# A two-layer hybrid decoder trunk on one core: head output of the MLA pairs in parts, rotary steps in other places, weight splits at another point of ScalarE's order

## The reference

```
h = rmsnorm(x, norm_g[l]) * (1.0 + scale) + shift
(a_q, a_f, a_i, a_g, b_cq, b_ckv, b_kr, b_g,
 c_q, c_k, c_v, c_g, m_a, m_b, m_c) = split_cols(h @ w_in[l])
y_a = hgrn2_mixer(a_q, a_f, a_i, ...) * silu(a_g)
y_b = mla_mixer(b_cq, b_ckv, b_kr, ...) * silu(b_g)
y_c = retention_mixer(c_q, c_k, c_v, ...) * silu(c_g)
merged = sigmoid(m_a) * (y_a @ w_pa[l]) + sigmoid(m_b) * (y_b @ w_pb[l]) + sigmoid(m_c) * (y_c @ w_pc[l])
x = x + gate * (merged @ w_out[l])
```

```
s = (qn @ k_nope^T + qr @ k_rope^T) * scale      # causal, 128 queries at a time
o = softmax(s) @ v
```

## Time and profile before

| | |
|---|---|
| median of 3 runs | 1367.94 us (1367.6 to 1369.93) |
| profiled execution | 1367.47 us |
| its span, first to last instruction | 1365.7 us |
| mean granted clock of TensorE | 0.977 of full speed |
| busy: PE, DVE, ACT, POOL | 94%, 51%, 46%, 53% |
| chain that ended last, by engine | PE 86%, DVE 7%, ACT 3%, issue 2% |

### The profile page before, as it was taken

How to read it: one execution, slowest core, us unless ns; L and a number is a source line. 1 busy time by engine, 2 the same in 40 slices (tenths; PEclk the granted TensorE clock), 3 DMA queues, 4 the chain that set the end, 5 groups by cost and what they waited for, 6 DMA issues and landing times.

```text
span 1365.7 us, 16803 instructions
## 1 busy us (share of the span) xinstructions
PE 1286.3 (94%) x5754; PEld 1013.3 (74%) x5754; DVE 698.4 (51%) x1136; ACT 626.6 (46%) x953; POOL 722.7 (53%) x1471
## 2 busy tenths in 40 slices
PE   5999999899789999999979999989979999999996
PEld 2878887777567777788858888777756687778884
DVE  6767767433655444454364777643354552433333
ACT  4276656434343244454235666544344424435431
POOL 3365555763324654576747654576522364555662
PEclk8999999999999999999989999999999999999998
DMA  9322223342113333233212212233211132232231
GB/s 374 118 84 77 63 67 104 112 146 90 48 62 108 130 102 108 101 124 105 95 55 93 78 62 71 70 99 120 90 47 39 56 130 75 87 99 87 93 93 62
DMA packets 40902, 130.51 MB, mean 96 GB/s; under 512 B 5392, under 2 KB 5520, under 8 KB 39536
## 3 DMA queue, kind: packets, MB, share of 16 engines
q1 hardware_dynamic: 30448, 110.22, 24.6%
q10 hardware_dynamic: 10368, 19.21, 4.4%
HBM read 126.33 MB, written 2.10 MB: 94 GB/s over the span
## 4 chain that ended last, share of the span: by engine, by line
PE 86%; DVE 7%; ACT 3%; issue 2%; POOL 1%; DMA 1%; ACTq 0%; DVEq 0%
PE ps_st L797 21%; PE ps_st L799 20%; PE ps_st L798 20%; PE ps_o L850 6%; PE ps_s L885 2%; PE ps_s L924 2%; PE ps_s L947 1%; PE ps_w L933 1%; POOL w_lo L669 1%; PE ps_misc L845 1%; ACT w_hi L1004 1%; DVE t L1298 1%; DVE neg_max L1709 1%; DVE gate_x L1315 1%; PE ps_w L752 1%
## 5 line engine op out<-in xcount | busy, mean ns | idle before, releaser
L669 POOL TENSOR_TENSOR w_lo<-raw,w_hi 128x128 fp32r<-128x128 f32 x1448 | 710.3, 529 | 602.6 <-ACT w_hi L1004 602.6
L797 PE MATMUL ps_st<-h_hi,w_hi 128*128 128x512 f32 x920 | 372.8, 405 | 2.7 <-POOL w_lo L669 2.2
L799 PE MATMUL ps_st<-h_hi,w_lo 128*128 128x512 f32 x920 | 359.0, 390 | 0.0
L798 PE MATMUL ps_st<-h_lo,w_hi 128*128 128x512 f32 x920 | 358.5, 390 | 0.0
L1004 ACT ACTIVATE w_hi<-raw 128x1024 fp32r<-128x1024 f32 x182 | 190.2, 1046 | 81.4 <-PE ps_st L799 51.9
L797 PEld LDWEIGHTS ps_st<-h_hi,w_hi 128*128 128x128 f32 x920 | 172.9, 188 | 44.8 <-issue 5.8
L798 PEld LDWEIGHTS ps_st<-h_lo,w_hi 128*128 128x128 f32 x920 | 173.0, 188 | 38.5 <-issue 4.8
L799 PEld LDWEIGHTS ps_st<-h_hi,w_lo 128*128 128x128 f32 x920 | 172.6, 188 | 36.9
L1315 DVE TENSOR_SCALAR gate_x<-ps_st 128x512 f32<-128x512 f32 x79 | 54.5, 690 | 219.7 <-PE ps_st L799 219.1
L1026 ACT ACTIVATE gate_t<-gate_x 128x512 f32<-128x512 f32 x80 | 50.5, 631 | 249.5 <-DVE gate_x L1315 249.5
L850 PE MATMUL ps_o<-mla_pt,v_ones 128*128 128x512 f32 (+3 forms) x128 | 46.4, 513 | 18.6 <-issue 10.2
(11 more groups left out here) (309 smaller groups left out, 2022.9 us busy)
## 6 DMA issues: line engine op xcount, KB each, us to landing
raw<-w_stream SPq DMA_DIRECT2D x178, 512.0 KB, 3.5
mod_w<-w_mod ACTq DMA_DIRECT2D x64, 256.0 KB, 2.7
pro_w<-w_mod_first SPq DMA_DIRECT2D x8, 1024.0 KB, 14.3
x<-x_t SPq DMA_DIRECT2D x4, 512.0 KB, 7.4
ret_decay<-decay ACTq DMA_DIRECT2D x2, 1024.0 KB, 5.0
out_t<-o_t SPq DMA_DIRECT2D x8, 256.0 KB, 2.2
raw<-w_stream SPq DMA_DIRECT2D x4, 384.0 KB, 3.2
raw_extra<-w_stream SPq DMA_DIRECT2D x2, 512.0 KB, 20.3
```

What stands on the lines that cost most here:

```text
L669: ins = nc.gpsimd.tensor_tensor(lo[:, r], whole[:, r], hi[:, r].bitcast(F32), ALU.subtract)
L797: nc.tensor.matmul(dst[0:m, :], wh, hi, start=(k == 0), stop=False)
L798: nc.tensor.matmul(dst[0:m, :], wh, lo, start=False, stop=False)
L799: last = nc.tensor.matmul(dst[0:m, :], wl, hi, start=False, stop=(k == nk - 1))
```

## The change

It has these parts.

1. `mixers_first` keeps the split in a list of its own and puts it out when the *next* group is flushed, behind that group's other steps.
2. `mla_pv` is cut for ScalarE and VectorE into `mla_rs` (rstd), `mla_y` (y_t; y_hi on odd heads) and `mla_lo` (y_lo). `mla_rs` of head h-1 stands between the third and fourth exponentials of head h, `mla_lo` behind the maxima of blocks 3 and 2 of a later head.
3. The odd key of a pair is copied in a step `mq_odd` of its own; the even key has a semaphore, `k_even`. PE waits for the even key before an even head's first score and for the odd key before the odd head's.
4. `mr` is read from its bank by a ScalarE copy into sq_sum, and turned by VectorE in a step `mr_rope`, for `mr 1` behind the maxima of head 3. `kr_rope` is done in two halves, one and two merge gates later.

```diff
@@ build_schedule
-    s += [("ckv_norm",), ("kr_rope",)]
-    for it in ma[1:-4]:
+    s.append(("ckv_norm",))
+    for n, it in enumerate(ma[1:-4]):
         item(*it)
+        if n < 2:
+            s.append(("kr_rope", n))
...
         else:
             item("bg", 0)
-        s += [("mla_t", h, 3), ("mla_t", h, 2), ("mla_s", h, 1), ("mla_s", h, 0)]
+        if h % 2 == 1 and h > 1:
+            s.append(("mla_lo", h - 2))
+        if h == 3:
+            s.append(("mr_rope", 1))
+        s += [("mla_t", h, 3), ("mla_t", h, 2)]
+        if h:
+            s += [("mla_rs", h - 1), ("mla_y", h - 1)]
+        s += [("mla_s", h, 1), ("mla_s", h, 0)]
         item(*behind[h])
         s += [("mla_t", h, 1), ("mla_t", h, 0)]
+        if behind[h][0] == "mq":
+            s.append(("mq_odd", behind[h][1]))
@@ mixers_first
-LATER = ("hg_v", "hg_out", "mla_pv", "ret_out")
+LATER = ("hg_v", "hg_out", "mla_y", "ret_out")
...
-            out += [t for t in group if t[0] not in EARLY + LATER + NEXT + ("item",)]
+            out += [t for t in group if t[0] not in EARLY + LATER + NEXT + ("item",)] + split
...
             if i < N_ITEMS and not (layer == 0 and RING - 1 <= i < len(BATCH)):
-                out.append(("split", ahead))
+                split = [("split", ahead)]
+            else:
+                split = []
@@ tensor, mla_s
-                        if e.new(q_ready, h // 2 + 1):
-                            pe.wait_ge(free[e.bank_of((("mq", h // 2), 0))], e.use(free, (("mq", h // 2), 0)))
-                            pe.wait_ge(free[e.bank_of((("mq", h // 2), 1))], e.use(free, (("mq", h // 2), 1)))
+                        pair = ("mq", h // 2)
+                        if qi == CH - 1 and h % 2 == 0:
+                            pe.wait_ge(free[e.bank_of((pair, 0))], e.use(free, (pair, 0)))
                             pe.wait_ge(q_ready, e.at(q_ready, h // 2 + 1))
+                            pe.wait_ge(k_even, e.at(k_even, h // 2 + 1))
+                        elif qi == CH - 1:
+                            pe.wait_ge(free[e.bank_of((pair, 1))], e.use(free, (pair, 1)))
@@ scalar
+                    elif kind == "mr":
+                        if j:
+                            act.wait_ge(q_ready, e.at(q_ready, 2 * j))
+                        copy_out((it, 0), sq_sum[:])
...
-                    elif kind == "mla_pv":
+                    elif kind == "mla_rs":
@@ vector
-                        V.tensor_copy(mla_kv[0:NOPE, 0, :], ps[0:NOPE, :])
-                        V.tensor_copy(mla_kv[NOPE:P, 1, :], ps[NOPE:P, :]).then_inc(free[e.bank_of((it, 1))], 1)
+                        V.tensor_copy(mla_kv[0:NOPE, 0, :], ps[0:NOPE, :]).then_inc(k_even, 1)
...
+                    elif kind == "mr_rope":
+                        key = (("mr", s[1]), 0)
+                        dve.wait_ge(free[e.bank_of(key)], e.use(free, key))
+                        mla_rope(sq_sum, range(P // ROPE)).then_inc(dve_link, 1)
+                        dve.wait_ge(dve_link, e.made(dve_link))
+                        V.tensor_tensor(sq_sum[:], t1[:], t2[:], ALU.add).then_inc(dve_link, 1)
+                        dve.wait_ge(dve_link, e.made(dve_link))
+                    elif kind == "mq_odd":
+                        key = (("mq", s[1]), 1)
+                        V.tensor_copy(mla_kv[NOPE:P, 1, :], bank[e.bank_of(key)][NOPE:P, :]).then_inc(free[e.bank_of(key)], 1)
+                    elif kind == "mla_lo":
+                        y_out(CH + s[1] // 2, y_hi[:, s[1] // 2, :], y_lo[:, s[1] // 2, :])
```

More of the change, by code:

```diff
@@ L54 @@
 TABLE_SET = "natural_log_exp_and_others"
-LINKS = {"act": 104, "dve": 36}
+LINKS = {"act": 104, "dve": 38}
 LEVELS = (64, 32, 16, 8, 4)
@@ L192, in build_schedule @@
         if it == ("rq", 1):
-            s.append(("mla_pv", MLA_HEADS - 1))
+            s += [("mla_pv", MLA_HEADS - 1), ("mla_rs", MLA_HEADS - 1), ("mla_y", MLA_HEADS - 1)]
+        if it == ("rk", 1):
+            s.append(("mla_lo", MLA_HEADS - 1))
     mb = merge_items("b")
@@ L319 @@
 EARLY = ("hz", "sel", "xb", "ex", "mod_acc")
-LATER = ("hg_v", "hg_out", "mla_pv", "ret_out")
+LATER = ("hg_v", "hg_out", "mla_y", "ret_out")
 NEXT = ("hg_rs",)
 def mixers_first(layer):
-    out, group, later, first, i = [], [], [], [], -1
+    out, group, later, first, split, i = [], [], [], [], [], -1
     for s in SCHEDULE[layer] + [("item",)]:
@@ L337, in mixers_first @@
             if i < N_ITEMS and not (layer == 0 and RING - 1 <= i < len(BATCH)):
-                out.append(("split", ahead))
+                split = [("split", ahead)]
+            else:
+                split = []
         else:
             group.append(s)
-    assert not later and not first
+    assert not later and not first and not split
     return out
@@ L1234, in _ @@
                         A(rstd[own, :], rstd[own, :], ACT.Exp, scale=-1.0).then_inc(rstd_ready, 1)
-                        if h % 2 == 1:
-                            pair = h // 2
-                            if pair == 0:
-                                act.wait_ge(full[e.bank_of((("pa", DT // 2 - 1), 1))], e.use(full, (("pa", DT // 2 - 1), 1)))
-                            act.wait_ge(y_t_ready, e.at(y_t_ready, CH + pair + 1))
-                            A(y_hi[:, pair, :], y_t[:], ACT.Copy).then_inc(y_hi_ready, 1)
+                    elif kind == "mla_y" and s[1] % 2 == 1:
+                        pair = s[1] // 2
+                        if pair == 0:
+                            act.wait_ge(full[e.bank_of((("pa", DT // 2 - 1), 1))], e.use(full, (("pa", DT // 2 - 1), 1)))
+                        act.wait_ge(y_t_ready, e.at(y_t_ready, CH + pair + 1))
+                        A(y_hi[:, pair, :], y_t[:], ACT.Copy).then_inc(y_hi_ready, 1)
                     elif kind == "mod_acc":
@@ L1377, in item @@
                                 lo_part(mg_lo[:, m, :], merged[:, m, :], mg_hi[:, m, :], mg_ready)
-                    elif kind == "mr":
-                        dve.wait_ge(full[e.bank_of((it, 0))], e.use(full, (it, 0)))
-                        mla_rope(bank[e.bank_of((it, 0))]).then_inc(free[e.bank_of((it, 0))], 1)
-                        dve.wait_ge(free[e.bank_of((it, 0))], e.use(free, (it, 0)))
-                        V.tensor_tensor(sq_sum[:], t1[:], t2[:], ALU.add).then_inc(dve_link, 1)
-                        dve.wait_ge(dve_link, e.made(dve_link))
                     elif kind == "mq":
@@ L1719, in _ @@
                         dve.wait_ge(free[e.bank_of(s)], e.use(free, s))
-                    elif kind == "mla_pv":
+                    elif kind == "mr_rope":
[10 more added lines that the diff above has]
+                        y_out(CH + s[1] // 2, y_hi[:, s[1] // 2, :], y_lo[:, s[1] // 2, :])
+                    elif kind == "mla_y":
                         h = s[1]
+                        key = ("mla_pv", h)
                         own = slice(0, MLA_DV) if h % 2 == 0 else slice(MLA_DV, P)
                         next_rstd()
-                        V.tensor_tensor(y_t[own, :], bank["o"][own, :], rstd[own, :], ALU.mult).then_inc(free[e.bank_of(s)], 1)
-                        dve.wait_ge(free[e.bank_of(s)], e.use(free, s))
+                        V.tensor_tensor(y_t[own, :], bank["o"][own, :], rstd[own, :], ALU.mult).then_inc(free[e.bank_of(key)], 1)
+                        dve.wait_ge(free[e.bank_of(key)], e.use(free, key))
                         if h % 2 == 1:
```

33 lines of the change are left out of this document (20 added, 13 removed).

## The result

| | before | changed |
|---|---|---|
| median of 4 runs each | 1367.77 us (1364.17 to 1369.93) | 1479.56 us (1476.16 to 1483.12) |
| ratio, 95% interval | | 1.082, 1.0785 to 1.0856 |
| profiled execution, its span | 1367.47, 1365.7 us | 1483.12, 1481.3 us |
| mean granted clock | 0.977 | 0.956 |

The changed kernel is 111.8 us slower; 1475 was forecast. That the total is so close is partly luck: it hides errors that cancel, as the experiments show.

What follows compares the result with a forecast made beforehand. TensorE, busy 94% of the span, was taken as the bound, so only its idle stretches and waits move the time. 1367.5 + 103 + 23 - 17 = 1476.5, given as 1475 us, range 1415 to 1535.

Steps and rivals of the forecast that it cites:

- Term 1: Item matmuls in all stages: weight rounding one item later makes PE wait for w_lo, 103 us.
- c merge and W_out: Stage of 20 items a layer: weights late by 0.6 to 3.1 us, 22 and 21 us for the two layers.
- `kr` to `ma 3`: Part of the a merge: subtractions end late beside VectorE's rotary work, net about 9 us a layer.
- The rule of one lateness for two items: Item chains: a PE stall delays a later chain too, so in steady state one lateness counts per two items.
- Term 2: TensorE clock: a little over half of some 25 waits of 1.9 us or more halve it, costing 23 us.
- Rival C: Clock stays full behind waits of 2 to 3 us: 1453 us; chance 0.12.
- Term 3: MLA heads: reordered rotary, rstd and key steps shorten PE's waits, -17 us, ends -10 and -24.
- Rotary of `mr 1`: MLA head 3: maxima now precede the rotary products, so PE's 5.1 us wait and clock loss go, gaining 11.
- `mla_rs` ahead of the last two exponentials: MLA heads: y_t no longer waits 2.04 us for rstd, exponentials come 1.2 later; 0 by itself.
- Rival D: Whole kernel faster: only the MLA gain shows, 1350 us; chance 0.03.
- A: Rival: ScalarE and VectorE catch up as PE stalls, so weight waits are 60 us, total 1415; chance 0.12.
- B: Rival: stalls feed one another, 137 us of waits, nearly every one halving the clock, total 1536; chance 0.12.

Runs made afterwards that it cites:

- e1: The changed kernel with the weight splits back at their old place, behind the work of item k-3, all else kept: 1337.11 us, ratio 0.9771.
- e10: The changed kernel with 336 useless TensorE products filling 31 of its long waits for w_lo: 1452.72 us, ratio 1.0628.
- e12: The kernel of e1 with 10 and 14 useless products in TensorE's two waits at the start of layer 1: 1338.04 us, ratio 0.9778.

## Why the prediction was right

The mechanism was right, and the first term nearly so in size. The second and third were each too small, by some 7 to 14 us and by 14, and cancelled: that part of the agreement is luck.

- **Term 1, 103 us of waits.** From e1 to the changed kernel idle time grows by 98.7 us. Waits for w_lo by stage, layers 0 and 1: c merge and W_out 17.8 and 16.2 (22 and 21 predicted), b merge 4.8 and 5.4 (5, 6), rest of the a merge 7.3 and 8.4 (7, 8), `kr` to `ma 3` 15.4 and 13.8 less the 4.0 that before had there (9, 9), HGRN 2.9 and 12.0 (7, 10), and 3.45 more in layer 0 with the wait of `cq 1`, one of the first items that the prediction had counted. Some 9 us more are hidden in the recorded ends (the estimate in the account), which the prediction had no term for. The rule of one lateness for two items is borne out: in the c merge `mc 0`, `mc 2`, `mc 3`, `pc 1` and `pc 2` wait, with others between them that don't. Two sizes were off most: the c merge and W_out 9 us too high, and `kr` to `ma 3` 3 us too low, where the subtractions of `ma 2`, counted nearer to 4.2, took 6.1 beside the rotary work.
- **Term 2, 23 us of clock.** 21 waits for w_lo of 1.9 us or more, for which 25 were assumed, and 13 have a low stretch behind them (0.62, for 0.55). But the stretches are longer than the 3.4 us taken: 65 us, a mean of 5.0, up to 10.2. Four more of 3.4 each stand elsewhere, three of them behind shorter waits and one behind the 3.45 of `cq 1`. Half of 78.5 is 39, less the 1.7 that e1 has in its place: 37.5. But PE was busy in only 63.9 of the 78.5 us, so the cost is 32 less 1.7, 30. The mis-sized step is twofold: 17 stretches for the 14 assumed, and 1.9 us a stretch for 1.7. e10 shows that it is indeed idle time that costs the clock, and that the column overstates the price.
- **Rival C** and the rule behind it are out: at full clock behind all waits the sum would have been 1453, and the changed kernel with its waits filled, where nothing but the clock improved, ran 1452.7. That these two agree is chance, since C had the gain 14 us too small and no term for the hidden time; what speaks against C is the 27 us between the changed kernel and e10. The Trainium skill ("TensorE: Matmul & The Clock Gate", section "Why this matters for your kernels") asks for gaps under about 3 us; this case's waits of 1.38 us before `pa 1` (at 294) and 1.74 before `cg 2` (at 564) have a granted 0.50 behind them, while those of 2.39 and 2.98 above had 1.00. As a bound on safe gaps the figure doesn't hold here. The two windows, changed kernel:

```profile
294.17:297.58 3.41, 3.41 (x8) 2.73 (x9) 0.00 (x0) 2.60 (x4) 1.64 (x4) 0.50 0.72 246
563.83:567.24 3.41, 3.41 (x8) 2.76 (x9) 0.00 (x0) 0.00 (x0) 3.27 (x8) 0.50 0.45 154
```

- **Term 3, -17 us.** Measured -31.5: 20.1 us of idle time for the 12 predicted, and 11.4 us of clock for the 5.1 that were counted. And its parts were put down wrongly. "Rotary of `mr 1`: 11" measured 0.7 alone. "`mla_rs` ahead of the last two exponentials: 0 by itself" measured 16.4 with y_lo. The step that failed is in the earlier trace rows itself: VectorE's y_t had waited 2.04 us for rstd, and I wrote that it no longer would, but priced that at nothing, because y_t itself was not urgent. What stood behind it in VectorE's queue was: rotary products, maxima and key copies. (How the 16.4 divide between rstd and y_lo is open.) `kr_rope` was put into term 1 with no number and gained 7.9.
- **Rival D** had the other half right: without part 1 the change gains. A (waits of 60 us) and B (137) are excluded by idle time near 100.

## What to carry to other kernels

Before moving a step later in an in-order queue, lay its whole chain (copy, subtraction, product: 7.1 us) against the cover it is left with (5.4 us) and sum the lateness over all rounds; here one list operation cost 142 us and hid a gain of 31 in the same change, so time the parts of a change apart. A wait of an engine off the critical path is priced by what is queued behind it and not by the instruction that waits: 2 us before an unhurried y_t, at nearly every head, were worth up to 16 together with the residual behind it. When idle time is removed the clock comes back too, worth about half as much again here (20 and 11 us). Where another engine paces the products, as at the layer boundary, a fuller clock gains nothing.

## What the chip showed besides

The clock at the start differs between executions of code that is the same there. Windows from 14 to 46 us of before, the changed kernel, e1 and e12:

```profile
14.00:46.00 32.00, 24.59 (x97) 16.67 (x97) 28.15 (x59) 14.34 (x16) 14.90 (x30) 0.79 0.79 317
```
```profile
14.00:46.00 32.00, 25.32 (x71) 16.63 (x71) 24.58 (x50) 12.79 (x14) 12.20 (x25) 0.57 0.78 310
```
```profile
14.00:46.00 32.00, 24.60 (x95) 16.61 (x95) 28.16 (x58) 14.33 (x16) 14.57 (x30) 0.79 0.80 316
```
```profile
14.00:46.00 32.00, 25.47 (x85) 16.89 (x86) 26.65 (x56) 13.68 (x16) 13.01 (x27) 0.68 0.79 312
```

Granted 0.57 instead of 0.79 over 32 us is 7 us of the changed kernel's profiled clock column, so of the 45.2 some 38 belong to the change (of the tighter 36.1 some 30); its profiled execution, 1483.1, was the slowest of four. e12's profiled one, 1342.2, stood 4 us above the others' 1336.8 to 1338.1. Differences under 5 us between single profiles of this kernel are thus to be read stage by stage.
